# Moving the gating stage of a hybrid attention and delta-rule block forward, and taking a lag out of its branch stage

## The reference, cut to what matters

```python
o_sb = from_heads(stick_breaking_attention(qa, ka, va)) * jax.nn.silu(sb_z)
o_dn = (rms_norm(o_dn, dn_norm_g) * jax.nn.silu(z_dn)).reshape(B, S, DN_WIDTH)
y = (jax.nn.sigmoid(merge_sb) * (o_sb @ w_branch_sb)
     + jax.nn.sigmoid(merge_dn) * (o_dn @ w_branch_dn))
out = y @ w_out
return x + gate[:, None] * out
```

## Time and profile before

| | us |
|---|---|
| median of 3 runs | 977.14 (976.19 to 978.98) |
| the profiled execution, its time | 977.48 |
| its span, first to last instruction | 975.5 |
| PE busy | 936.0 (96%) |
| DVE busy | 535.9 (55%) |
| ACT busy | 322.6 (33%) |
| POOL busy | 219.1 (22%) |

### The profile page before, as it was taken

How to read it: one execution, slowest core, us unless ns; L and a number is a source line. 1 busy time by engine, 2 the same in 40 slices (tenths; PEclk the granted TensorE clock), 3 DMA queues, 4 the chain that set the end, 5 groups by cost and what they waited for, 6 DMA issues and landing times.

```text
span 975.5 us, 13734 instructions
## 1 busy us (share of the span) xinstructions
PE 936.0 (96%) x5507; PEld 785.1 (80%) x5507; DVE 535.9 (55%) x773; ACT 322.6 (33%) x732; POOL 219.1 (22%) x130
## 2 busy tenths in 40 slices
PE   3799999999999999999999999999999999999998
PEld 3688889878888778888888888888888778887886
DVE  4776999698886344554043274133335547645322
ACT  7542222487886322112621111223223641110000
POOL 0003414430000121121334111100011117672000
PEclk9999999999999999999999999999999999999999
DMA  9950513510220212111313436311112874435321
GB/s 318 249 176 22 161 36 109 148 40 17 61 50 17 74 44 64 44 44 38 93 47 116 133 106 168 92 44 54 44 45 86 298 242 129 130 123 201 104 90 65
DMA packets 122665, 100.55 MB, mean 103 GB/s; under 512 B 18055, under 2 KB 104672, under 8 KB 122346
## 3 DMA queue, kind: packets, MB, share of 16 engines
q1 hardware_dynamic: 92298, 76.07, 26.1%
q10 hardware_dynamic: 30304, 23.60, 8.0%
HBM read 73.44 MB, written 24.12 MB: 100 GB/s over the span
## 4 chain that ended last, share of the span: by engine, by line
PE 80%; DVE 7%; ACT 3%; POOL 3%; DMA 3%; issue 3%; SPq 0%; ACTq 0%; DVEq 0%
PE psum L822 41%; PE psum L269 5%; PE psum L271 5%; PE psum L270 5%; PE psum L657 5%; PE psum L1068 3%; PE psum L1051 3%; DMA sg<-z_scratch 3%; DVE stick L1167 3%; PE psum L659 2%; PE psum L1403 1%; POOL hlo L2008 1%; PE psum L1037 1%; PE psum L1039 1%; POOL sg L2017 1%
## 5 line engine op out<-in xcount | busy, mean ns | idle before, releaser
L822 PE MATMUL psum<-hhi,w3hl 128*128 128x512 f32 x1120 | 365.6, 396 | 3.9 <-issue 3.2
L822 PEld LDWEIGHTS psum<-hhi,w3hl 128*128 128x128 f32 x1120 | 210.3, 188 | 48.1 <-issue 5.4
L822 PE MATMUL psum<-hlo,w3hl 128*128 128x512 f32 x560 | 218.3, 390 | 0.0
L811 POOL TENSOR_TENSOR w3hl<-w3raw,w3hl 128x1024 fp32r<-128x1024 f32 x43 | 102.7, 2389 | 467.2 <-DVE w3hl L804 467.2
L822 PEld LDWEIGHTS psum<-hlo,w3hl 128*128 128x128 f32 x560 | 105.4, 188 | 20.0
L1167 DVE TENSOR_TENSOR_SCAN stick<-stick,floor 128x1024 f32<-128x1024 f32 (+7 forms) x64 | 91.0, 1466 | 15.1 <-ACT stick L1115 14.6
L822 PE MATMUL psum<-ohi,w3hl 128*128 128x512 f32 x256 | 80.2, 394 | 2.4 <-issue 2.4
L804 DVE CAST w3hl<-w3raw 128x1024 fp32r<-128x1024 f32 x43 | 35.3, 820 | 71.4 <-DMA w3raw<-in_w_in 41.4
L906 ACT COPY zst<-psum 128x512 f32<-128x512 f32 x44 | 25.9, 589 | 130.3 <-PE psum L822 124.5
L657 PE MATMUL psum<-w,hhi 128*128 128x512 f32 x192 | 67.5, 396 | 0.0
L822 PEld LDWEIGHTS psum<-ohi,w3hl 128*128 128x128 f32 x256 | 48.9, 191 | 13.0 <-issue 2.8
(11 more groups left out here) (232 smaller groups left out, 1580.9 us busy)
## 6 DMA issues: line engine op xcount, KB each, us to landing
z_scratch<-zst ACTq DMA_DIRECT2D x44, 256.0 KB, 2.2
w3raw<-in_w_in ACTq DMA_DIRECT2D x20, 512.0 KB, 4.3
ada<-in_ada_w SPq DMA_DIRECT2D x16, 512.0 KB, 6.3
w3raw<-in_w_in SPq DMA_DIRECT2D x16, 512.0 KB, 4.0
sg<-z_scratch SPq DMA_DIRECT2D x8, 1024.0 KB, 5.0
xrow<-in_x SPq DMA_DIRECT2D x4, 1024.0 KB, 6.3
w1raw<-in_w_in SPq DMA_DIRECT2D x4, 1024.0 KB, 7.1
adag<-in_ada_w SPq DMA_DIRECT2D x8, 512.0 KB, 4.2
```

The costliest lines, as they stand in the source:

```text
L811: nc.gpsimd.tensor_tensor(lo, w3raw[:], cast(hi), ALU.subtract).then_inc(w3_lo, 1)
L822: t = nc.tensor.matmul(out_, a[:, kt, :], moving[b][:, kt, 512 * half:512 * half + 512], start=(ends[0] and kt == k0 and m == 0), stop=(en ...
```

## The change

1. **Gates earlier.** `load_gating` is called two half tiles earlier (`AHEAD = 2`), and its first step waits only for the delta rule's last uses of the memory that it overwrites, not for the phase's end. The loads of gates 4 and 5 wait for one more use; the load of `w7raw` waits for the phase's end and also comes two half tiles earlier. ACT makes the SiLU of gates 0 and 1 before the last half tile of phase 4, and the high parts of 0 and 1 and the SiLU of 2 and 3 after the turned copies. DVE makes gates 0 and 1 and their low parts at the end of phase 4.
2. **`left`.** What is left of gates 2 and 3 now stands **before** the pieces of half tile 42, gates 4 to 7 behind half tiles 42 and 43.
3. **Turning among pieces.** After each `turn_output(r)` PE runs one piece of half tile 42; the drain follows all eight.
4. **Branch stage.** DVE casts `high(n)` and POOL makes `low(n)` in half `n` itself, not in `n + 1`.

```diff
             for m in range(2 * F2, 2 * NF):
-                load_gating(sp, m - AFTER)
+                load_gating(sp, m - (AFTER - AHEAD))
...
             for r in range(ST):
                 turn_output(r)
+                z_piece(pe, KT * AFTER + r)
             pe.drain().then_inc(phase_end, 1)
-            for n in range(KT * AFTER, NPIECES):
+            for n in range(KT * AFTER + ST, NPIECES):
                 z_piece(pe, n)
...
             rsqrt_out()
+            silu_z(act, 0)
+            silu_z(act, 1)
             z(AT_TAIL, AT_TAIL + TAIL)
             for r in range(ST):
                 copy_out_t(r)
+            for i in range(2):
+                high_part(act, i)
+            silu_z(act, 2)
+            silu_z(act, 3)
             act.drain().then_inc(phase_end, 1)
...
             normalize_out()
             z(AT_TAIL, AT_TAIL + TAIL)
+            for i in range(2):
+                gated(dve, i)
+            for i in range(2):
+                low_part(dve, i)
             dve.drain().then_inc(phase_end, 1)
...
+        AHEAD = 2
 
         def left(one_half, gating):
 
             for m in range(AFTER, 2 * NF):
+                if m == AFTER:
+                    gating(2)
+                    gating(3)
                 for n in range(KT * m, KT * m + KT):
                     one_half(n)
-                if m - AFTER < ZT:
-                    gating(2 * (m - AFTER))
-                    gating(2 * (m - AFTER) + 1)
+                if m - AFTER < ZT // 2:
+                    gating(ZT + 2 * (m - AFTER))
+                    gating(ZT + 2 * (m - AFTER) + 1)
...
             if step == 0:
-                sp.wait_ge(phase_end, 5 * 3 + 4)
+                sp.wait_ge(g["Y"], ST)
+                sp.wait_ge(g["KS"], ST)
+                sp.wait_ge(g["ktr"], ST)
                 for s_ in z_out:
                     sp.wait_ge(s_, 16 * 2 * ZT)
+            if step == ZT // 2:
+                sp.wait_ge(g["AV"], ST)
+            if step == ZT:
+                sp.wait_ge(phase_end, 5 * 3 + 4)
...
             def gate_act(i):
-                silu_z(i)
+                if i >= ZT:
+                    silu_z(act, i)
                 if i % 2:
-                    high_part(i - 1)
-                    high_part(i)
+                    high_part(act, i - 1)
+                    high_part(act, i)
...
                     nc.vector.tensor_tensor(v, v, br_bank(i, branch, half), ALU.mult).then_inc(tg_ok, 1)
-                if n >= 1:
-                    high(n - 1)
+                high(n)
                 if n in (2, 4):
                     split_w7(dve, n // 2 - 1)
-            high(2 * KT - 1)
...
                 nc.gpsimd.tensor_tensor(a, a, b, ALU.add).then_inc(yt_ok, 1)
-                if n >= 1:
-                    low(n - 1)
-            low(2 * KT - 1)
+                low(n)
```

More of the change, by code:

```diff
@@ L1892, in load_gating, with silu_z @@
                 sp.dma_start(w7raw[0][:, kts], wout_v[:, kts, 0:512]).then_inc(w7_in[0], 16)
-        def act_5(act):
[L1895 to L1901, removed]
+        def silu_z(act, i):
+            act.wait_ge(z_in[i % ZT], 32 if i < ZT else 48)
+            nc.scalar.activation(zraw[:, i, :], zraw[:, i, :], ACT.Silu).then_inc(zs_silu, 1)
@@ L1903, in gate_act, with high_part @@
+        def high_part(act, i):
+            act.wait_ge(g_ok, i + 1)
+            nc.scalar.copy(ohi[:, i, :], zraw[:, i, :]).then_inc(ohi_ok, 1)
+        def act_5(act):
             def gate_act(i):
-                silu_z(i)
+                if i >= ZT:
+                    silu_z(act, i)
                 if i % 2:
-                    high_part(i - 1)
-                    high_part(i)
+                    high_part(act, i - 1)
+                    high_part(act, i)
             left(lambda n: copy_z(act, n), gate_act)
-        def dve_5(dve):
[L1912 to L1917, removed]
-                    nc.vector.scalar_tensor_tensor(out=v, in0=dnT[:, i - ZT, :], scalar=paramT[:, V_DG:V_DG + 1],
-                                                   in1=v, op0=ALU.mult, op1=ALU.mult).then_inc(g_ok, 1)
-            def low_part(i):
-                dve.wait_ge(ohi_ok, i + 1)
-                nc.vector.tensor_tensor(olo[:, i, :], zraw[:, i, :], cast(ohi[:, i, :]), ALU.subtract).then_inc(olo_ok, 1)
@@ new lines, in gated @@
+        def gated(dve, i):
+            dve.wait_ge(zs_silu, i + 1)
+            v = zraw[:, i, :]
+            if i < ZT:
+                nc.vector.tensor_tensor(v, oraw[:, i, :], v, ALU.mult).then_inc(g_ok, 1)
+            else:
+                if i == ZT:
+                    dve.wait_ge(g["aOT"], ST)
+                nc.vector.scalar_tensor_tensor(out=v, in0=dnT[:, i - ZT, :], scalar=paramT[:, V_DG:V_DG + 1],
+                                               in1=v, op0=ALU.mult, op1=ALU.mult).then_inc(g_ok, 1)
@@ L1925, in gate_dve, with low_part @@
+        def low_part(dve, i):
+            dve.wait_ge(ohi_ok, i + 1)
+            nc.vector.tensor_tensor(olo[:, i, :], zraw[:, i, :], cast(ohi[:, i, :]), ALU.subtract).then_inc(olo_ok, 1)
+        def dve_5(dve):
             def gate_dve(i):
-                gated(i)
+                gated(dve, i)
                 if i % 2:
-                    low_part(i - 1)
-                    low_part(i)
+                    low_part(dve, i - 1)
+                    low_part(dve, i)
             left(lambda n: next_hi(dve, n), gate_dve)
```

## The result

The changed kernel takes 980.42 us (median of 7 runs, 979.36 to 982.53) against 977.28 (7 runs, 973.76 to 978.98): ratio 1.0038, 95% interval 1.0022 to 1.0054. It is slower, clear of noise, by 3.1 us. The forecast was 985.7, 8.6 us slower than the 977.14 that it started from. The sign and the places of PE's new waits were right, the size was about 2.7 times too large.

The account below looks back on a forecast made before the run. PE was taken to wait for DVE's and POOL's weight splits. Branch stage start 797.4, plus 95.3 branch stage, 87.5 last projection and 3.96 end, gave 984.2; plus 1.98, less 0.34: 985.7 us, range 977.5 to 991.0.

Parts of the forecast that it names:

- Bound and method: From the delta rule's end: PE waits for weight splits by DVE and POOL, decided by the cast's place in DVE's list.
- Part 1: Eight turns among pieces: 3.5 us of turns against 6.24, gain 2.3 us; PE ends tile 33 at 766.5.
- Part 2: Gating stage: a new 6.2 us wait before tile 34; branch stage starts 3.65 us later; 2.3 lost net with part 1.
- ACT's chain behind the last copy: Gating stage: after ACT's last copy at 760.7, high parts 0 and 1 at 1.1 us each, SiLUs 2 and 3 to 765.0.
- (d): Rival: as forecast, plus the clock falling at each of four waits and gate loads colliding: 989 to 993 us; chance 0.12.
- Part 3: Branch stage without lag: waits of 4 and 2 us before fourth and fifth tiles, stage 7.8 over 87.5; last projection's 1.57 gone.
- the chain from cast to cast: Branch stage: DVE takes 9.2 us per tile, 14.8 in two tiles with last weights' splits, 3.9 over PE's time.
- the prediction's lower bound: Branch stage: per-tile chain is 13.7 us if the weight cast keeps 0.69 alone, taking 3.3 off tile 40.
- the chain's start: Branch stage: merge gates load at T + 4.0, multiplications start at T + 11.2, tile 38's cast comes at T + 17.7.
- (a): Rival: only the gating order bites, DVE and POOL keep up in the branch stage: to 978.0 us; chance 0.08.
- (b): Rival: only the branch stage bites, gates 0 to 3 done before PE ends tile 33: to 977.0 us; chance 0.06.
- (c): Rival: faster, both engines keep up in both places and PE's three idle times are won: to 969.2 us; chance 0.06.

Follow-up runs that it names:

- branch-only: Kernel before with only the branch stage's lag taken out (high and low parts made in half n itself): 979.38 us, ratio 1.0025.
- turning-only: Kernel before with one fill piece behind each turn and nothing else: 977.91 us, ratio 1.0012.
- front-only run: Changed kernel with the branch stage's lag put back, leaving turning among pieces and earlier gates: 978.79 us, ratio 1.0018.
- the one with both edits: Changed kernel with weight casts ahead of gates, loads and copies sooner, and the last weights' splits moved to the gating stage's end: 967.73 us, ratio 0.9907.
- cast 34 and copy 42 moved: Changed kernel with DVE's cast of tile 34 between gates 1 and low part 0, ACT's copy of half tile 42 ahead of high parts: 979.87 us, 1.0021.
- cast 34 first: Changed kernel with DVE's cast of tile 34's weights moved ahead of gates 0 and 1: 981.31 us, ratio 1.0041.

## Why the prediction was right or wrong

**Bound and method: right.** What PE waits for is the weight splits, and their lateness is a matter of order in DVE's list. With casts, copies and loads in the order of their deadlines the gating stage came out 8.1 us shorter.

**Part 1: right.** Turn r begins 1.13 us after turn r - 1 (750.01, 751.15, 752.28 in PE's timeline), no idle time in between. PE reached the end of tile 33 at 765.05, 15.04 after the first turn; the forecast had 15.0.

**Part 2: right in place, 1.2 us over in size.** The wait before tile 34 was forecast at 6.2 and was 5.39; POOL's low part was ready 20.3 us after the first turn, forecast 21.0. The step that was off is ACT's chain behind the last copy. It took high parts and SiLUs at 1.0 us each, and began the first high part 0.2 us earlier after the first turn than forecast:

```profile
759.03 2.00 ACT L1921 CAST ohi<-zraw 128x1024 fp32r<-128x1024 f32 x2
760.93 2.00 ACT L1917 ACTIVATE zraw<-zraw 128x1024 f32<-128x1024 f32 x2
```

The 1.1 us of the earlier trace rows was taken from a pair whose second high part had waited for its gate. Tile 35's wait was forecast at about 1.3 with the slow clock (785.0 against 786.3) and was 0.38. The clock did fall after 5.4 us of idleness, and the loss was hidden in that wait, as said: tile 34 took 783.36 - 770.44 = 12.92 us. The changed kernel's windows:

```profile
766.00:772.80 6.80, 2.36 (x6) 1.91 (x7) 6.67 (x6) 3.73 (x6) 2.34 (x1) 0.61 0.58 193
842.00:844.80 2.80, 2.74 (x8) 2.15 (x9) 1.57 (x3) 0.00 (x0) 2.26 (x2) 0.59 0.58 170
```

Two sentences of this part were wrong and cost nothing. The load of tile 34's weights did not slip behind the SiLUs: ACT's queue issued it at 746.15, ahead of SiLUs that stand before it in the list and started at 747.68. And its cost was not nothing by itself: it took 9.7 us instead of 4.2, with the moved gate loads beside it. Only the late cast hid that. The forecast's sum had no term for it; of the rivals only (d) names gate loads that collide.

**Part 3: right in place, 2.7 us over in size; this is the term that failed.** The waits stand before the fourth and fifth tiles as forecast, 1.33 and 2.06 us for 4 and 2 (T is again the start of the branch stage; tile 39 ready at T + 34.0 for 36.7, tile 40 at T + 47.3 for 51.5). Two terms of the sum were too large.

The first is the chain from cast to cast, put at 14.8; it took 13.3. The last weights' cast took 1.22, not 2.31, and each addition 1.28, not 1.47. Both durations of the earlier trace rows were those of an instruction that began beside a busy neighbour. In the new order the other engine begins second and pays. POOL's rows of the changed kernel beside the casts at 811.29 and 817.12:

```profile
811.46 1.68 POOL L2030 TENSOR_TENSOR hlo<-sg,hhi 128x512 fp32r<-128x512 f32 x1 [0.54 <-DVE hhi L2012]
...
817.28 2.21 POOL L2030 TENSOR_TENSOR hlo<-sg,hhi 128x512 fp32r<-128x512 f32 x1 [0.54 <-DVE hhi L2012]
```

The same low part takes 1.30 where DVE is quiet. The chain's first term was right by luck. It was put at 1.78 for the weight cast beside POOL; the cast took 0.69, and what keeps POOL from its split of the weights is the first of these rows, the low part of the half before, which the sum did not have (811.29 to 813.10, 1.81 us). For that reason the prediction's lower bound, 13.7, taken for a cast of 0.69, did not hold either: the cast did take 0.69, the term stayed at 1.8, and the chain was below the bound.

The second is the chain's start: the cast of tile 38 was put at T + 17.7 and came at T + 16.6 (811.29 - 794.70), since the first merge gates were loaded 3.4 us into the stage (798.13), not 4.0, and the two additions ahead of it took 1.29 and 1.30 us, not 1.47.

Together they put tile 40 4.2 us too late. About 1.5 of that came back as slow clock behind the fifth tile's wait, which the sum had only among its bounds (45.25 us from 842.06 to the last projection, for 4 x 10.93), hence 2.7.

The cause was right in part. The round trip costs what the prediction says it does, a wait of DVE at each high cast, and it takes 2.1 to 2.3 us from the chain's start. But it does not make the chain between casts longer than the lag does (13.2 and 12.6), where DVE waits for merge gates instead, and the prediction's answer to why the splits do not hurt today was too easy: with the lag and the splits in the stage, PE waited 1.4 us before the fifth tile in three other kernels (1.39, 1.40, 1.38). What decides is the last weights' splits: out of the stage, they take PE's waits with them.

What the prediction gave for the last projection was right as a time (87.2 us, no wait). Its reason holds where the splits are in the stage: each of the four kernels with the lag has the wait there (1.57, 0.39, 0.65, 0.84), and none without it has. It is not the only way, since with the splits early the wait is gone with the lag kept.

One reading of the shown rows was short: the earlier trace rows has the multiplications' 1.28 us in a row that begins with POOL idle. The statement stands by another row of that trace, 812.05, where they take 1.29 beside POOL's split. And the sum's terms add to 985.8, not 985.7.

**The rule on the shared port.** The Trainium skill (GPSIMD Engine Reference, Specifications) has GpSimd's SBUF interface shared with VectorE. The trace agrees here too, with 1.30 against 2.21 us for one operation. What the sum needed besides is which of the two pays. In these traces it was the one that started second.

**The rest of the gap** between 8.6 and 3.1 us is 0.3 us in the last stretch and 1.5 between the parts ahead of the first turn, 1.25 of which is the slow clock at 39 to 43 in the profile of the kernel before. Single profiles cannot say how much of the medians' 3.1 it is, since what lies ahead of the first turn varied by 3.3 us over the twelve profiles. Whether the kernel before's profile, with 1.3 us lost to a slow clock at 793.75, is typical of its runs also stays open; the branch-only and the turning-only profile had the same idle time there (2.32 and 2.36) without that loss.

**Rivals.** (a), only the gating order bites, falls by the branch-only run; (b) by the front-only run. (c), nothing bites, decided at a cast of tile 34 ready by 763.4 (it began at 767.2) and fell. (d) falls by the time; of its parts, the loads did run into each other, hidden behind the late cast, and the clock fell behind two of the four waits (5.39 and 2.06). A kernel as dense as (c) exists, the one with both edits, and its time, 967.7, is within 1.5 us of the 969.2 that was worked out for (c): what was missing was the order of casts, copies and loads, and another place for the splits.

## What to carry to other kernels

When one engine is busy 96% of the time, a stage is won or lost by where the small helper instructions that it waits for stand in the other engines' lists: put the cast, copy or load with the nearest deadline ahead of bulk work, and look in every list, since the next late one takes over (here DVE's cast, then ACT's copy, then the next tile's cast). Work that fits anywhere, as the last weights' splits, belongs where its engine idles, not into the stage that already runs close to the bound. A duration taken from a row holds for the order of that row: if the neighbour that slowed it will now start second, take the quiet row.

## What the runs showed of the hardware

- After 2.36 us of idleness before the branch stage TensorE's clock was granted at 0.59 of full speed in the kernel before, near 1.2 of 2.4 GHz, and stayed at 1.00 after 2.32 and 2.36 us at the same place of two other kernels. After 2.06 us before the fifth branch tile it was 0.59 in the changed kernel and 1.00 with the branch part alone. After 3.35 us it fell in one profile and not in the other (39 to 43 us), after 3.53 us (turning only) it stayed, after 3.69 (cast 34 and copy 42 moved) it fell to 0.50, and after 4.73 and 5.39 it fell each time. So idle times of 2 to 3.7 us cost themselves, and 1.3 to 1.7 us more only in some runs.
- Two operations of DVE and POOL that contend did not share evenly here. The one that started second took most of the delay: POOL's low part 1.30 us alone, 1.68 and 2.21 behind a cast of DVE; DVE's cast 0.69 alone, 1.78 behind POOL.
- A 512 KB load of weights took 4.2 us to land with no gate load under way, and 9.7 and 11.8 us where four gate loads of the same size were issued on SP's queue within 1 us of it and two more some 4.7 us later.
- ACT's queue issued a DMA ahead of activations that stand before it in the list: at 746.15 for a load behind two SiLUs that started at 747.68, and at 747.06 against 748.59 in the run with cast 34 first.
